# A two-block network on one core: two output features begun inside the last attention items, the first norm's sum moved, and turned attention weights of five item groups kept in float32

## The reference

```python
def dsa_mixer(h, w_in, q_g, k_g, iq_g, ik_g, w_out):      # h = rms_norm(x, norm_mix_g[0])
    proj = h @ w_in            # q: 8 heads of 128; c: 128; qi: 8 heads of 64; ki: 64; wi: 8
    ki = rms_norm(ki, ik_g);  wi = wi * (8 ** -0.5 * 64 ** -0.5)
    q = rms_norm(q, q_g) * (128 ** -0.5);  k = rms_norm(c, k_g);  qi = rms_norm(qi, iq_g)
    # for each block of 128 queries:
    rel = jax.nn.relu(einsum('bqhd,bsd->bqhs', qi, ki));  score = einsum('bqhs,bqh->bqs', rel, wi)
    score = where(key < limit, score, -inf);  _, idx = lax.top_k(score, 128)
    logits = einsum('bqhd,bqkd->bqhk', q, k[idx]);  p = softmax(logits over admissible keys)
    o = einsum('bqhk,bqkd->bqhd', p, c[idx])
    return o @ w_out
x = x + dsa_mixer(...)
```

## Time and profile before

| | before |
|---|---|
| time, median of 3 runs | 2215.22 us (2212.89 to 2218.27) |
| the profiled execution: its time, its span | 2217.77 us, 2216.0 us |
| TensorE busy (matmuls) | 2170.4 us, 98% |
| TensorE weight loads | 1797.5 us, 81% |
| VectorE, ScalarE, GpSimd busy | 1187.9, 897.7, 919.7 us (54%, 41%, 42%) |
| DMA | 200.43 MB, mean 90 GB/s |
| granted TensorE clock, mean | 0.992 |

### The profile page before, as it was taken

One profiled execution on the slowest core, in us unless ns is written; L12 is line 12 of the kernel. 1 busy time (PEld: TensorE's weight loads), 2 busy tenths in 40 slices (PEclk: granted clock), 3 DMA queues, 4 the chain that ended last, 5 costly groups with the idle time before them and its releaser, 6 DMA issues.

```text
span 2216.0 us, 25698 instructions
## 1 busy us (share of the span) xinstructions
PE 2170.4 (98%) x10002; PEld 1797.5 (81%) x10002; DVE 1187.9 (54%) x1835; ACT 897.7 (41%) x1306; POOL 919.7 (42%) x438
## 2 busy tenths in 40 slices
PE   7989999999999999999999999999999999999999
PEld 6877888888888888888888888887777788888887
DVE  6883476444345253465763533997556423765351
ACT  6454444332333323344442324434656434443231
POOL 2423444444443333433444444644322454444443
PEclk9999999999999999999999999999999999999999
DMA  3101232322322222222322224321111232322232
GB/s 131 67 20 52 87 103 95 105 88 98 114 87 90 91 83 83 87 78 86 105 95 96 95 95 157 106 76 67 67 58 58 86 133 88 102 98 100 91 105 95
DMA packets 57657, 200.43 MB, mean 90 GB/s; under 512 B 6400, under 2 KB 7168, under 8 KB 57280
## 3 DMA queue, kind: packets, MB, share of 16 engines
q1 hardware_dynamic: 57536, 198.79, 26.7%
HBM read 194.30 MB, written 4.19 MB: 90 GB/s over the span
## 4 chain that ended last, share of the span: by engine, by line
PE 86%; DVE 7%; ACT 4%; issue 3%; DMA 0%; POOL 0%; SPq 0%; DVEq 0%; ACTq 0%; POOLq 0%
PE ps L314 26%; PE ps L316 26%; PE ps L315 26%; DVE ps L2001 2%; PE ps L342 2%; PE ps L344 2%; PE ps L343 2%; PE ps L357 1%; PE ps L1136 1%; ACT WH L285 1%; PE ps L388 0%; DMA WS<-in_w 0%; DVE SC L2158 0%; DVE SC L2161 0%; ACT SC L1920 0%
## 5 line engine op out<-in xcount | busy, mean ns | idle before, releaser
L295 POOL TENSOR_TENSOR WL<-WS,WH 128x1024 fp32r<-128x1024 f32 (+2 forms) x362 | 854.9, 2363 | 1194.7 <-ACT WH L285 1194.7
L314 PE MATMUL ps<-H,WH 128*128 128x512 f32 (+1 forms) x1776 | 700.7, 395 | 9.7 <-DVE H L472 9.7
L316 PE MATMUL ps<-H,WL 128*128 128x512 f32 (+1 forms) x1776 | 695.1, 391 | 0.0
L315 PE MATMUL ps<-H,WH 128*128 128x512 f32 (+1 forms) x1776 | 694.9, 391 | 0.0
L285 ACT ACTIVATE WH<-WS 128x1024 fp32r<-128x1024 f32 (+2 forms) x362 | 374.6, 1037 | 441.5 <-PE ps L316 343.6
L314 PEld LDWEIGHTS ps<-H,WH 128*128 128x128 f32 (+1 forms) x1776 | 335.4, 189 | 82.1 <-POOL WL L295 8.3
L316 PEld LDWEIGHTS ps<-H,WL 128*128 128x128 f32 (+1 forms) x1776 | 335.0, 189 | 71.9 <-issue 0.6
L315 PEld LDWEIGHTS ps<-H,WH 128*128 128x128 f32 (+1 forms) x1776 | 335.4, 189 | 67.6 <-issue 0.4
L314 PE MATMUL ps<-G,WH 128*128 128x512 f32 x880 | 344.4, 391 | 1.5 <-DVE G L1445 1.5
L315 PE MATMUL ps<-G,WH 128*128 128x512 f32 x880 | 343.4, 390 | 0.0
L316 PE MATMUL ps<-G,WL 128*128 128x512 f32 x880 | 343.4, 390 | 0.0
(11 more groups left out here) (234 smaller groups left out, 2021.1 us busy)
## 6 DMA issues: line engine op xcount, KB each, us to landing
WS<-in_w SPq DMA_DIRECT2D x337, 512.0 KB, 3.2
WS<-in_w SPq DMA_DIRECT2D x24, 384.0 KB, 3.1
X<-in_x SPq DMA_DIRECT2D x8, 256.0 KB, 5.6
xs<-X SPq DMA_DIRECT2D x1, 2048.0 KB, 9.0
X<-xs SPq DMA_DIRECT2D x8, 256.0 KB, 5.5
out<-X SPq DMA_DIRECT2D x8, 256.0 KB, 2.9
X<-in_sg SPq DMA_DIRECT2D x1, 1344.0 KB, 5.6
SC<-in_rot SPq DMA_DIRECT2D x4, 256.0 KB, 3.7
```

What stands on the lines that cost most here:

```text
L295: e.tensor_tensor(lo, raw, hi.bitcast(F), ALU.subtract).then_inc(*P.sig("w_lo", i))
L314: e.matmul(out, lh, rh, start=start, stop=False)
L315: e.matmul(out, lh, rl, start=False, stop=False)
L316: return e.matmul(out, ll, rh, start=False, stop=stop)
```

## The change

Line numbers behind it are higher by 4 to 38. Its parts:

1. `aiq` 0 is computed in one piece; the norm's sum comes behind it and behind `weights_turn`.
2. ScalarE's program begins with the load of an activation table that has the square root as well as copies and squares. (In the instructions, the load before the first square root is gone.)
3. For the groups 0 to 4 (items 0 to 19) the turned weights are written once, unrounded, and not cut: `low` does nothing, and `values` is one float32 matmul for each key tile instead of three fp32r ones. They have 1, 3, 2, 3 and 4 key tiles. The c operand is kept whole in `SC` beside its two parts, instead of in a buffer of `TMP`. The PSUM bank of a turned item is now free after ScalarE's copy.
4. Output features 0 and 1 begin in the last steps: half of feature 0 (heads 0 to 3) four steps before the end, half of feature 1 behind the last `values`, and then both second halves.
5. Some tensors get a second name in float32 over the same memory, with aligned starts.

```diff
+def d_whole(k):
+    return k // 4 < 5
+def d_pt_whole(P, k):
+    qb, _, place = D_GROUPS[k // 4]
+    z = {"A": P.whole("G", 9216, 2048), "B": P.whole("G", 13312, 1024), "H": P.whole("H", 0, 2048)}[place]
+    return z[:, 0:512 * (qb + 1)].rearrange("p (k c) -> p k c", k=qb + 1)
+def d_c_whole(P):
+    return P.sc(S0 + 2816)
@@ pe_dsa
-    half_feature(P, e, ("aiq", 0), P.hs(), lambda: pe_sum(P, e, "nm0"))
+    feature(P, e, ("aiq", 0), P.hs())
     weights_turn()
+    pe_sum(P, e, "nm0")
@@ pe_dsa, values
-        e.wait_ge(*P.at("p_lo", k))
+        e.wait_ge(*P.at("p_hi" if d_whole(k) else "p_lo", k))
         if k == 3:
+            e.wait_ge(*P.at("c_scaled"))
+        if k == 23:
             e.wait_ge(*P.at("c_lo"))
         for kt in range(qb + 1):
+            cc = slice(128 * kt, 128 * kt + 128)
+            if d_whole(k):
+                t = e.matmul(o, d_c_whole(P)[:, cc], d_pt_whole(P, k)[:, kt, :], start=kt == 0, stop=kt == qb)
+                continue
...
+    outputs = [(d_q(P, k, 0), d_q(P, k, 1)) for k in range(8)]
+    outs = [out_steps(m) for m in range(2)]      # half_steps(P, e, ("aout", m), outputs, 4)
     for n in range(D_STEPS):
...
+        if n == D_STEPS - 4:
+            e.wait_ge(*P.at("o_lo", (3, 0)))
+            next(outs[0])
         d_items(n, (3, turn), (6, values))
+    next(outs[1])
+    e.wait_ge(*P.at("o_lo", (0, 1)))
+    for out in outs:
+        next(out)
     P.longest_free = False
-    for m in range(8):
-        feature(P, e, ("aout", m), [(d_q(P, k, 0), d_q(P, k, 1)) for k in range(8)],
-                ready=(lambda k: [("o_lo", (0, 1))] if k == 0 else []) if m == 0 else None)
+    for m in range(2, 8):
+        feature(P, e, ("aout", m), outputs)
@@ act_dsa, cut
-        hi = d_pt(P, k, 0)[:, :, 128 * hh:128 * hh + 128]
+        hi = (d_pt_whole(P, k) if d_whole(k) else d_pt(P, k, 0))[:, :, 128 * hh:128 * hh + 128]
...
         e.activation(hi, src, ACT.Copy).then_inc(*P.sig("p_hi", k))
+        if d_whole(k):
+            P.end["ps", ("tn", k)] = ("p_hi", k)
@@ dve_dsa, low
+        if d_whole(k):
+            return
@@ act_program
+    e.preload_act_table_set("sqrt_and_others")
```

More of the change, by code:

```diff
@@ L196, in cut, with whole @@
         return self.m[name, R][:, a:a + n]
+    def whole(self, name, a, n=T):
+        return self.m[name, F][:, a:a + n]
     def H(self, k, lo):
@@ L1129, in logits, with out_steps @@
             *P.sig("logits", k))
+    def out_steps(m):
+        return half_steps(P, e, ("aout", m), outputs, 4)
     def turn(k, qb, h):
@@ L1143, in values @@
         o = bank(P, e, ("vl", qb, s))
-        e.wait_ge(*P.at("p_lo", k))
+        e.wait_ge(*P.at("p_hi" if d_whole(k) else "p_lo", k))
         if k == 3:
+            e.wait_ge(*P.at("c_scaled"))
+        if k == 23:
             e.wait_ge(*P.at("c_lo"))
         for kt in range(qb + 1):
+            cc = slice(128 * kt, 128 * kt + 128)
+            if d_whole(k):
+                t = e.matmul(o, d_c_whole(P)[:, cc], d_pt_whole(P, k)[:, kt, :], start=kt == 0, stop=kt == qb)
+                continue
             r = [d_pt(P, k, z)[:, kt, :] for z in (0, 1)]
-            cc = slice(128 * kt, 128 * kt + 128)
             t = mm3(e, o, d_c(P, 0)[:, cc], d_c(P, 1)[:, cc], r[0], r[1], kt == 0, kt == qb)
         t.then_inc(*P.sig("values", k // 4))
+    outputs = [(d_q(P, k, 0), d_q(P, k, 1)) for k in range(8)]
+    outs = [out_steps(m) for m in range(2)]
     for n in range(D_STEPS):
@@ L1238, in act_dsa @@
     e.wait_ge(*P.at("c_scaled"))
-    e.activation(d_c(P, 0), P.TMP(P.slot_of("TMP", ("ct",))), ACT.Copy).then_inc(*P.sig("c_hi"))
+    e.activation(d_c(P, 0), d_c_whole(P), ACT.Copy).then_inc(*P.sig("c_hi"))
     query(2)
@@ L1397, in dve_dsa @@
     step(2)
-    i, prev = P.take("TMP", 2, ("ct",))
-    if prev is not None:
-        e.wait_ge(*P.freed("TMP", prev))
     e.wait_ge(*P.at("c_turn"))
-    tmp = P.TMP(i)
-    e.tensor_tensor(tmp.rearrange("p (j c) -> p j c", j=4), P.ps(("ct",)).rearrange("p (j c) -> p j c", j=4),
+    e.tensor_tensor(d_c_whole(P).rearrange("p (j c) -> p j c", j=4), P.ps(("ct",)).rearrange("p (j c) -> p j c", j=4),
                     P.m["SM"][:, 492:496].unsqueeze(2).to_broadcast([128, 4, 128]), ALU.mult).then_inc(*P.sig("c_scaled"))
     P.end["ps", ("ct",)] = ("c_scaled", None)
-    P.end["TMP", ("ct",)] = ("c_lo", None)
     step(10)
@@ L1483, in pool_dsa @@
     e.wait_ge(*P.at("c_hi"))
-    e.tensor_tensor(d_c(P, 1), P.TMP(P.slot_of("TMP", ("ct",))), d_c(P, 0).bitcast(F), ALU.subtract).then_inc(
-        *P.sig("c_lo"))
+    e.tensor_tensor(d_c(P, 1), d_c_whole(P), d_c(P, 0).bitcast(F), ALU.subtract).then_inc(*P.sig("c_lo"))
     query(2)
@@ L2405, in program @@
                             ("SM", 508, F)):
-            at = nc.sbuf_base
+            at = (nc.sbuf_base + 31) // 32 * 32
             mem[name] = ctx.enter_context(nc.sbuf_tensor(name, [128, n], dt))
@@ L2409, in program @@
                 mem[name, R] = nc.alloc_sbuf_tensor_at(name + "_cut", [128, n], R, offset=at)
+            if name in ("H", "G"):
+                mem[name, F] = nc.alloc_sbuf_tensor_at(name + "_whole", [128, n], F, offset=at)
         mem["banks"] = [ctx.enter_context(nc.psum_tensor(f"ps{i}", [128, T], F))[:, :] for i in range(8)]
```

## The result

The changed kernel takes 2209.04 us (median of 8 runs, 2207.87 to 2211.71) against 2215.48 (8 runs, 2212.74 to 2218.27): by the medians 6.4 us or 0.29% less. The ratio, estimated over all runs, is 0.9976 (95% interval 0.9967 to 0.9984), that is 5.3 us (3.5 to 7.3). The forecast was 2208.7.

What follows compares the result with a forecast made beforehand. TensorE, busy 98% of the span, was taken as the bound. Parts 1 to 4 summed as +0.2 + 0 - 0.5 - 6.2 = -6.5 us, giving 2208.7 us against 2215.22, range 2205.0 to 2214.5.

Steps and rivals of the forecast that it cites:

- wait and gate: Start: TensorE waits over 2 us at the first pair's statistics; a 0.67 us wait at 40.93 gives back earlier gains.
- the landmark: Start: the index matmul of the second pair, at 40.93 before, was to come at 40.5 to 41.5.
- the term for the new slow stretch: Start, work from 31.4 on: new idle time may lower the clock again, costing 1.7 us like the present slow stretch.
- the forecast +0.2: Part 1, at the start: net loss of 0.2 us, range 0 to +0.6.
- the start gains: Rival: the gate at 40.93 gives way and 2.9 us come on top, total 2205.8; chance 0.06.
- the longer gap: Part 2, start: first four inputs' products 1.3 us earlier, so TensorE idles longer before the second half, maybe at low clock.
- the rule on the faster weight loads: Part 3: faster weight loading is off for float32; by the rule 4.9 us added, by the trace nothing.
- VectorE's lead at V: VectorE's first logits of 512 columns, at 150.45 before: removed low parts save 2.26 us of VectorE's time.
- 1.7 us of lead at the next logits: Part 3: TensorE's lead left after group 2's two whole products at low clock; groups 3 and 4 take 1.2.
- the bounds of -2.2 to +1.3: Part 3, forecast -0.5 us net: -2.2 if the clock is high, +1.3 if passes cost 0.28 and low clock lasts longer.
- O - T: Part 4, drain from the last turn's two records to the third output feature: forecast -6.2 us, range -2.0 to -6.5.
- the profiled execution's surplus of 2.55 us: Sum: the profiled execution lay 2.55 us above the runs' median, so 2211.3 against it became 2208.7 against 2215.22.

Runs made afterwards that it cites:

- part 4 alone: Kernel before with only output features 0 and 1 begun inside the last items: 2210.38 us, ratio 0.9981.
- part 3 alone: Kernel before with only the turned weights of groups 0 to 4 whole in float32: 2215.30 us, ratio 1.0007.
- the second profile of the kernel before: Kernel before, unchanged, profiled again: median 2214.88 us, ratio 1.0004; the profiled execution took 2217.08.
- the early load: Weight unit of the start asked for one step earlier, ahead of the wait for the key features' low part; in the changed kernel 2207.54 us, ratio 0.9960.
- parts 1 and 2 alone: Kernel before with only the norm's sum moved and the table load at ScalarE's program start: 2215.01 us, ratio 1.0003.
- the early load alone: Kernel before with only the start's weight unit asked for one step earlier: 2212.95 us, ratio 0.9996.
- both edits with the sum at its old place: Changed kernel with weight unit asked for earlier and only groups 0 to 2 whole, but part 1 undone: 2207.50 us, ratio 0.9968.
- 3 groups whole: Changed kernel with only groups 0 to 2 whole in float32, groups 3 and 4 split again: 2208.69 us, ratio 0.9964.
- parts 1 to 3: Changed kernel with part 4 undone, all output features after the loop: 2215.63 us, ratio 1.0003.
- both edits: Changed kernel with the start's weight unit asked for one step earlier and only groups 0 to 2 whole in float32: 2205.97 us, ratio 0.9964.
- either timing of the whole: Changed kernel timed in two sets of runs: 2209.04 us, ratio 0.9976, and 2210.08 us, ratio 0.9972.

## Why the prediction was right, point by point

**Part 1: right in kind, wait and gate as said; the landmark missed.** A wait of 2.29 us at the statistics (2 to 3 forecast), no wait at the sum. The index matmul came at 41.94, outside 40.5 to 41.5. The step that failed is the term for the new slow stretch, 1.7 us as the one of now: the clock was low from 29.8 to 36.7, twice as long as the 3.4 us at 21.7. From the statistics to the index matmul it took 12.27 us instead of 9.96, of which 0.67 were a wait, so the low clock cost 2.98. Less the 1.30 by which the statistics start earlier and the 0.67 that is the +1.01 of the ledger. But a slow stretch stands there without part 1 too: from 30.8 to 37.6 with part 4 alone (I at 42.57), from 32.8 to 36.2 with part 3 alone (41.51), from 31.2 to 34.7 in the second profile of the kernel before. Over the traces without the early load I is 40.22 to 42.57 without part 1 (4 of them) and 41.30 to 42.96 with it (6). A loss of the forecast +0.2 or of 0.7 can't be told apart there; the time of parts 1 and 2 alone, +0.4 us with an interval of -1.3 to +2.4, doesn't decide it either. The rival "the start gains" is out: its 2.9 us appear nowhere. The gate shows without part 1 as well: with part 4 alone, which has no slow stretch at 22, TensorE waits 0.87 us at 30.30 for the same square. What the prediction did not see is that the slow stretch is not tied to the wait that it took away: with part 4 alone and with the early load alone TensorE waits 1.01 and 1.21 us at 20.6 for the same sum, and no low clock follows before 30.

**Part 2: right.** No table load near 22.5, nothing gained that shows. The first product comes at 7.01 instead of 8.35, and the longer gap that was named as its danger did come: in two of the nine traces with part 2 (parts 1 and 2, and both edits with the sum at its old place) TensorE waited 1.81 and 2.03 us at 13.7 to 14.0 instead of 0.91, and the clock was low soon after, from 15.1 to 18.5 and from 14.3 to 17.6. Waits of 1.64 and 1.78 us there in two others had none behind them.

**Part 3: each price right, the lead added up wrong.** Product: 0.164 us more (0.17 forecast), also with weight loads of float32. By the rule on the faster weight loads named in the prediction (Trainium skill, TensorE: Matmul & The Clock Gate, Weight-path perf modes) 7 products would have cost 7 x (0.17 + 2 x 0.19) = 3.9 us, as an estimate; the traces with 3 and 5 groups differ by 1.15, so nothing of such a cost shows for these. VectorE's lead at V: 2.03 (2.26 forecast). The first whole product of group 2 was forecast at 149.8; less the 1.57 of the stretch at 104, which this trace lacks, plus the 1.01 by which I is later, that is 149.2; it is at 149.34. Low clock there: as forecast.

The step that failed is "1.7 us of lead at the next logits". It doesn't follow from the prediction's own numbers: TensorE is 151.55 - 149.8 = 1.75 us ahead at the first product, the two whole products at the low clock cost 3.4 - 2.6 = 0.8 more, and 0.95 is left (a little more if the clock rises sooner). Groups 3 and 4 cost 1.2, so the part should have been forecast at about +0.2, not -0.5. That is what the traces show: the kernels with 3 groups whole keep 139.58 - 138.59 = 1.0 of lead, groups 3 and 4 take 1.15 of it, and the net is +0.2, well inside the bounds of -2.2 to +1.3.

Step by step, the changed kernel against the one with part 4 alone, each counted from its I: the turn of item 14 (148.57 and 150.91) starts 1.71 us earlier. It waits for GpSimd's diagonal, which follows VectorE's reciprocal, as the prediction said. The first product with c (149.34 and 152.18) starts 2.21 us earlier, and the second matmul of the logits behind it (152.96 and 154.61) 1.02 us earlier. Between the last two the changed kernel needs 3.62 us and the other 2.43; 3.3 and 1.6 of them are at 1.2 GHz. So 1.2 us of the lead go in the two whole products at the low clock.

**Part 4: right in the trace, smaller in the medians.** O - T went from 18.13 to 11.82, -6.31 (forecast -6.2), third feature at 193.51 (about 193.9). Waits of 1.68 and 1.50, units there in time, the outputs' low part covered: all as forecast. But 2.7 us of the sum were the low clock at 186.8, counted as belonging to the kernel before. Traces without part 4 have O - T of 18.1 (three), 17.1 (two) and 15.5 (one): the part is worth 6.3, 5.3 or 3.7, depending on where the clock is low in that execution. Part 4 alone gave 4.2 in the medians. The profiles say the same in whole times: the three with a stretch at 104 and one of 7 us at 186 took 2217.1 to 2218.1, the two of part 3 and of parts 1 to 3, with none at 104 and some 3 us at 186, 2215.4 and 2216.4, the one with neither 2210.3. The runs of the kernels with part 4 spread over 2 to 5 us (both edits: 7), those without it over 4 to 8.

**The sum.** -6.5 forecast, -6.4 measured by the medians (-5.3 by the ratio). The agreement is closer than its parts: +0.2, -0.5 and -6.2 stand against about +0.4, +0.7 and -4.2 for the parts timed alone, each with 1 to 2 us of uncertainty, and their sum, -3.1, is less than either timing of the whole (-6.4, and -4.9 by the medians of the second). Where those 2 to 3 us come from, chance or the clock's stretches, the runs don't settle. The two traces differ by 9.0 us where 6.5 were forecast: 1.6 of it is the stretch at 104 and 2.1 the clock behind the late float32 matmul, neither of which any part explains. Taking the profiled execution's surplus of 2.55 us off the sum worked by luck: it was in all likelihood made of such stretches, and the one at 186 among them is in the price of part 4 as well, so it was counted and taken off again.

## What to carry to other kernels

Fill the waits of a drain with work that is ready: it gains the waits for certain and the low clock that may follow them in some executions only, so count the two apart. When an engine gets ahead, follow the lead through the next instructions of the other engine, at the clock that it has there: here TensorE was 2.2 us ahead at two products and 1.0 behind them. Before a wait is removed, see which transfer the next wait ends on: moving the sum gave nothing in any trace, and asking for that load one step earlier moved the index matmul by 1.95 us, though its gain in time, 1.5 to 2.5 us, is not shown beyond its interval.

## What the runs showed of the hardware that was not expected

- The granted clock falls to 1.2 GHz in stretches of 3 to 4 or of about 7 us, and one program has them in different places: the kernel before at 22 to 25 in one profile and at 31 to 35 in the other. The stretch of 7 us stood at 30 to 37 (after), 185 to 192 (before) or 144 to 151 (before with the early load). What it costs is decided by whether TensorE has work under it: 3.4 us at 104 cost 1.57 (109.54 against 107.97, and 107.53 against 105.96).
- A stretch need not follow a visible wait directly: in the window 103:107 of before TensorE is busy for 4.00 of 4 us at 0.58. The last wait ahead of it, 1.37 us, ended at 101.27, and the clock fell at 103.6. The same wait, 1.36 to 1.38 us at 100.5 to 102.9, stands in the changed kernel, in that with part 4 alone and in that with the early load alone, and no low clock follows there.
- Seven whole float32 products of 512 columns cost 1.15 us more than their 21 fp32r matmuls: some 0.85 us for a float32 product of two records against 0.68 for the split in three.
- An operation on four elements per partition can take VectorE 2.30 us, and 0.16 us otherwise (in the kernel before 2.35 at 31.75); in the changed kernel, ahead of it GpSimd's row:

```profile
28.63 4.68 POOL L299 TENSOR_TENSOR WL<-WS,WH 128x1024 fp32r<-128x1024 f32 x2 [5.93 <-ACT WH L289]
```

```profile
31.02 2.30 DVE L426 TENSOR_TENSOR SM<-SM 128x4 f32<-128x4 f32 x1
33.35 0.16 DVE L428 TENSOR_TENSOR SM<-SM 128x4 f32<-128x4 f32 x1
```

The slow one ends at 33.32, and GpSimd's second low part of weights at 33.31. That the one waits for the other was not tried.
